# Sums of squares of the differential half in two single-pass matmuls over a split square

## What is computed

```python
def _rmsnorm(x, g):
    xf = x.astype(jnp.float32)
    y = xf * lax.rsqrt(jnp.mean(xf * xf, axis=-1, keepdims=True) + EPS)
    return (y * g.astype(jnp.float32)).astype(x.dtype)
...
    qd = _rmsnorm(df_q.reshape(b, s, DF_HEADS, 2, DF_HEAD_DIM), q_norm_g)
    kd = _rmsnorm(df_k.reshape(b, s, DF_HEADS, 2, DF_HEAD_DIM), k_norm_g)
...
    df_o = _diff_attention(q1, q2, k1, k2, vd, lam, _alibi_slopes(DF_HEADS))
    df_o = _rmsnorm(df_o, subln_g) * (1.0 - lam_init)
    df_out = _from_blocks(df_o) * jax.nn.silu(df_g.astype(jnp.float32))
```

## Time and profile before

| what | value |
|---|---|
| median of 3 runs | 1531.65 us (1530.02 to 1531.93) |
| the profiled execution | 1531.95 us |
| its span in the profile | 1530.2 us |
| TensorE busy | 1477.6 us |
| VectorE busy | 957.4 us |
| ScalarE busy | 671.5 us |

### The profile page before, as it was taken

How to read it: one execution, slowest core, us unless ns; L and a number is a source line. 1 busy time by engine, 2 the same in 40 slices (tenths; PEclk the granted TensorE clock), 3 DMA queues, 4 the chain that set the end, 5 groups by cost and what they waited for, 6 DMA issues and landing times.

```text
span 1530.2 us, 20100 instructions
## 1 busy us (share of the span) xinstructions
PE 1477.6 (97%) x7076; PEld 1156.4 (76%) x7076; DVE 957.4 (63%) x1464; ACT 671.5 (44%) x1085; POOL 66.5 (4%) x123
## 2 busy tenths in 40 slices
PE   5999899999999999999989999999999999999988
PEld 5876678888888887666767888888888766667767
DVE  6644667777776647545446777777777654456662
ACT  6544444444442225344443444444332355555661
POOL 1100000000001120000000000000111011100000
PEclk9999999999999999999999999999999999999999
DMA  6222223322236632111212322223576411111221
GB/s 239 97 69 70 83 84 107 96 96 96 96 116 222 237 126 83 67 45 42 69 42 83 110 96 96 96 96 111 199 247 212 134 55 55 56 56 55 70 97 56
DMA packets 42899, 159.16 MB, mean 104 GB/s; under 512 B 4884, under 2 KB 5140, under 8 KB 42840
## 3 DMA queue, kind: packets, MB, share of 16 engines
q1 hardware_dynamic: 33480, 126.40, 24.7%
q0 software_dynamic: 8208, 29.89, 5.9%
q10 hardware_dynamic: 1152, 2.10, 0.4%
HBM read 156.27 MB, written 2.10 MB: 103 GB/s over the span
## 4 chain that ended last, share of the span: by engine, by line
PE 86%; DVE 6%; ACT 5%; issue 2%; DMA 0%; SPq 0%; ACTq 0%; DVEq 0%
PE ps L348 18%; PE ps L350 17%; PE ps L349 17%; PE ps L364 7%; PE ps L366 7%; PE ps L365 7%; PE ps L451 2%; PE ps L521 2%; DVE wl L282 1%; PE ps L509 1%; ACT wh L276 1%; PE ps L1741 1%; DVE rbc L445 1%; PE ps L1731 1%; PE ps L1756 1%
## 5 line engine op out<-in xcount | busy, mean ns | idle before, releaser
L276 ACT CAST wh<-raw 128x1024 fp32r<-128x1024 f32 (+1 forms) x213 | 234.5, 1101 | 283.0 <-PE ps L350 247.4
L282 DVE TENSOR_TENSOR wl<-raw,wh 128x1024 fp32r<-128x1024 f32 (+1 forms) x213 | 273.3, 1283 | 99.4 <-ACT wh L276 99.2
L348 PE MATMUL ps<-xh,wh 128*128 128x512 f32 x728 | 284.3, 391 | 1.7 <-DVE wl L282 1.7
L350 PE MATMUL ps<-xh,wl 128*128 128x512 f32 x728 | 283.3, 389 | 0.0
L349 PE MATMUL ps<-xl,wh 128*128 128x512 f32 x728 | 283.2, 389 | 0.0
L364 PE MATMUL ps<-xh,wh 128*128 128x512 f32 x448 | 191.8, 428 | 2.5 <-DVE wl L282 2.5
L366 PE MATMUL ps<-xh,wl 128*128 128x512 f32 x448 | 176.3, 394 | 0.0
L365 PE MATMUL ps<-xl,wh 128*128 128x512 f32 x448 | 175.9, 393 | 0.0
L348 PEld LDWEIGHTS ps<-xh,wh 128*128 128x128 f32 x728 | 136.6, 188 | 31.1 <-DVE wl L282 2.5
L349 PEld LDWEIGHTS ps<-xl,wh 128*128 128x128 f32 x728 | 136.6, 188 | 28.9 <-issue 0.5
L350 PEld LDWEIGHTS ps<-xh,wl 128*128 128x128 f32 x728 | 136.6, 188 | 28.3
(11 more groups left out here) (271 smaller groups left out, 2152.0 us busy)
## 6 DMA issues: line engine op xcount, KB each, us to landing
raw<-w_a_f SPq DMA_DIRECT2D x44, 512.0 KB, 3.2
raw<-w_b_f SPq DMA_DIRECT2D x44, 512.0 KB, 3.2
row<-w_c_rows POOLq DMA_DIRECT2D x32, 512.0 KB, 4.6
row<-w_ada_rows POOLq DMA_DIRECT2D x24, 512.0 KB, 4.8
raw<-w_a_f SPq DMA_DIRECT2D x16, 704.0 KB, 4.1
raw<-w_b_f SPq DMA_DIRECT2D x16, 704.0 KB, 4.4
raw<-w_b_pair SPq DMA_DIRECT2D x18, 512.0 KB, 3.2
raw<-w_sb SPq DMA_DIRECT2D x16, 512.0 KB, 3.3
```

The source lines that it names most:

```text
L276: nc.scalar.copy(wh[:, s, :width], raw[:, s, :width]).then_inc(w_hi, 1)
L282: nc.vector.tensor_tensor(wl[:, s, :width], raw[:, s, :width], wh[:, s, :width].bitcast(F32), ALU.subtract).then_inc(w_lo, 1)
L348: nc.tensor.matmul(dst, a, h(k), start=(k == 0), stop=False)
L350: mm = nc.tensor.matmul(dst, b, h(k), start=False, stop=(k == total - 1))
```

## The change

The square is copied once more by ScalarE into a tile of type fp32r (`sqh`), VectorE subtracts that from the square into another (`sql`, `square_low`), and TensorE makes two fp32r matmuls, one over each, added in PSUM. The ones and the block of ones are copied into fp32r once (`plus`), on ScalarE ahead of unit 0. `square_low` stands in VectorE's order at the step of the sum: at step 0 behind the reductions, at step 4 behind L1411 and ahead of the split, at step 6 behind the reductions (or clamps, in unit 3) and ahead of the split; for the last output, behind unit 7. TensorE waits for it (`lo`) in place of the square (`sq`).

```diff
--- before.py
+++ after.py
@@ -189,6 +189,9 @@
         ptd = at("ptd", [P, 2, S], F32, 70)
         osb = at("osb", [P, S], F32, 74)
         sqd = at("sqd", [P, S], F32, 76)
+        sqh = at("sqh", [P, S], F32R, 46)
+        sql = at("sql", [P, S], F32R, 48)
+        plus = at("plus", [P, 2 * P], F32R, 54)
         ogt = at("ogt", [P, S], F32, 78)
         kal = at("kal", [68, 5 * S], BF16, 80)
         rfn = at("rfn", [P, S], F32, 85)
@@ -232,7 +235,8 @@
         c_b, c_e, c_l, c_sp, c_sc, c_p = (sem("c_" + n) for n in ("b", "e", "l", "sp", "sc", "p"))
         b_vt, b_vn = sem("b_vt"), sem("b_vn")
         sbs = {n: sem("sb_" + n) for n in ("z", "min", "e", "ln", "sp", "tri", "a", "u", "pv")}
-        dfs = {n: sem("df_" + n) for n in ("sq", "ss", "ln", "r", "n", "o1", "o2", "qg")}
+        dfs = {n: sem("df_" + n) for n in ("sq", "hi", "lo", "ss", "ln", "r", "n", "o1", "o2", "qg")}
+        k_plus = sem("k_plus")
         l_vt, l_vn, l_si, l_o, l_pr = sem("l_vt"), sem("l_vn"), sem("l_si"), sem("l_o"), sem("l_pr")
         n_x2, n_h, n_hs = sem("n_x2"), sem("n_h"), sem("n_hs")
         y_out = [sem("y_out0"), sem("y_out1")]
@@ -940,9 +944,11 @@
             act.wait_ge(ada_mod, 4)
             rounds(act, "b_f2", 4, 4, split_hi, body)
 
-            def squares(src, s_ready, v_ready):
+            def squares(k, src, s_ready, v_ready):
                 act.wait_ge(s_ready, v_ready)
                 nc.scalar.activation(sqd[:, :], src, ACT.Square).then_inc(dfs["sq"], 1)
+                act.wait_ge(dfs["sq"], k + 1)
+                nc.scalar.copy(sqh[:, :], sqd[:, :]).then_inc(dfs["hi"], 1)
 
             def unit(n, k, src=st):
 
@@ -957,10 +963,10 @@
                 n, i, p = C0["sb"] + 4 * u + l, u - 4, u % 2
                 split_hi(act, n + 2, n + 2)
                 if i >= 0 and l == 0:
-                    squares(kts[:, p, :], l_pr, 3 * u + 1)
+                    squares(n_k(i), kts[:, p, :], l_pr, 3 * u + 1)
                 if i >= 0 and l == 1:
                     unit(HD, n_k(i))
-                    squares(qts[:, p, :], l_pr, 3 * u + 2)
+                    squares(n_q(i), qts[:, p, :], l_pr, 3 * u + 2)
                 if l == 3:
                     act.wait_ge(l_vt, u + 1)
                     unit_pv(act, u - 2)
@@ -988,6 +994,8 @@
                 return f
 
             project(0, 0)
+            nc.scalar.copy(plus[:, 0:P], ones).then_inc(k_plus, 1)
+            nc.scalar.copy(plus[:, P:2 * P], bdiag).then_inc(k_plus, 1)
             norm_root(act, 5, rbc[:, :], bias=sm[:, 60:61])
             norm_root(act, 6, rfn[:, :])
             table(EXP_LN_SET)
@@ -1047,7 +1055,7 @@
                 act_pairs(exps, copy, behind_last(u))
                 if u < 7:
                     project(u + 1, 3)
-                squares(osb[:, :], dfs["o1"], u - 3)
+                squares(n_o(u - 4), osb[:, :], dfs["o1"], u - 3)
             unit(P, n_o(3), lg[0])
             mix_high(act, 7, MIXC + 7, ogt[:, :], l_o, 8)
 
@@ -1392,6 +1400,11 @@
                     nc.vector.scalar_tensor_tensor(kts[:, p, :], kts[:, p, :], col("k_norm_g_2"), drb[:, :],
                                                    ALU.mult, ALU.mult).then_inc(dfs["n"], 1)
 
+            def square_low(k):
+
+                dve.wait_ge(dfs["hi"], k + 1)
+                nc.vector.tensor_tensor(sql[:, :], sqd[:, :], sqh[:, :].bitcast(F32), ALU.subtract).then_inc(dfs["lo"], 1)
+
             def output(i):
 
                 k = n_o(i)
@@ -1410,6 +1423,12 @@
                             norm_factor(dve, 6, rfn[:, :])
                         nc.vector.scalar_tensor_tensor(xt[:, u, :], xt[:, u, :], col("final_norm", u), rfn[:, :],
                                                        ALU.mult, ALU.mult).then_inc(n_x2, 1)
+                    if u > 4 and t == 0:
+                        square_low(n_o(u - 5))
+                    if 3 <= u < 7 and t == end_step(0, 4) + 2:
+                        square_low(n_k(u - 3))
+                    if 3 <= u < 7 and t == end_step(1, 4) + 2:
+                        square_low(n_q(u - 3))
                     if u > 4 and t == 1:
                         output(u - 5)
                     if u > 4 and t == 2:
@@ -1488,6 +1507,7 @@
                 if u < 7:
                     project(u + 1, 3)
                     split(u + 1, 3)
+            square_low(n_o(3))
             output(3)
             mix_low(dve, 7, MIXC + 7, ogt[:, :])
 
@@ -1660,9 +1680,12 @@
                     pe.wait_ge(dfs["ln"], n_q(u - 4) + 1)
                 turn(pe, st, vts[:, :], l_pr, 3 * u + 3).then_inc(l_vt, 1)
 
+            ones_r, bdiag_r = plus[:, 0:P], plus[:, P:2 * P]
+
             def sums(k, m, dst=st):
-                pe.wait_ge(dfs["sq"], k + 1)
-                nc.tensor.matmul(dst[:, :], m, sqd[:, :], start=True, stop=True).then_inc(dfs["ss"], 1)
+                pe.wait_ge(dfs["lo"], k + 1)
+                nc.tensor.matmul(dst[:, :], m, sqh[:, :], start=True, stop=False)
+                nc.tensor.matmul(dst[:, :], m, sql[:, :], start=False, stop=True).then_inc(dfs["ss"], 1)
 
             OUT_EARLY = ([(j, k) for j in range(2) for k in range(6)] + [(0, 6), (1, 6)] +
                          [(j, k) for j in (2, 3) for k in range(7)])
@@ -1699,12 +1722,13 @@
                         for i in range(2 * t, 2 * t + 2):
                             out_block(*OUT_EARLY[i])
                     if u > 4 and t == 0:
-                        sums(n_o(u - 5), ones)
+                        sums(n_o(u - 5), ones_r)
                     if 3 <= u < 7 and t == end_step(0, 4) + 2:
                         pe.wait_ge(l_vn, u + 1)
-                        sums(n_k(u - 3), bdiag)
+                        pe.wait_ge(k_plus, 2)
+                        sums(n_k(u - 3), bdiag_r)
                     if 3 <= u < 7 and t == end_step(1, 4) + 2:
-                        sums(n_q(u - 3), bdiag)
+                        sums(n_q(u - 3), bdiag_r)
                 return f
 
             job(pe, [(C0["sb"], C0["sb"], KD)], J0["sb"], J0["sb"], X, XL, ready=(x_lo, X0["sb"]))
@@ -1804,7 +1828,7 @@
             for i in range(20, 23):
                 out_block(*OUT_EARLY[i])
             pe.wait_ge(att["df"]["exp"], 32)
-            sums(n_o(3), ones, lg[0])
+            sums(n_o(3), ones_r, lg[0])
             for i in range(23, 28):
                 out_block(*OUT_EARLY[i])
             for j in range(4):
```

## The result

The changed kernel takes 1541.10 us (median of 4 runs, 1538.97 to 1542.93) against 1531.79 for the kernel before: ratio 1.0061, 95% interval 1.0044 to 1.0077, so slower by 9.3 us. The forecast was slower, 1537.4 us, range 1533.8 to 1540.5. The direction was right and the size too small: the median lies 0.6 us above the range. The four runs lie in two pairs, 1538.97 and 1539.52 with a mean granted clock of 0.994, 1542.68 and 1542.93 with 0.991. The profiled execution is the fastest, 1538.97 us with a span of 1537.0.

What follows compares the result with a forecast made beforehand. TensorE's own queue was taken to set the pace. Terms of 0.9 + 3.8 + 0.4 + 0 + 0.6 gave +5.7 us; 1531.95 + 5.7 - 0.3 made 1537.4 us, range 1533.8 to 1540.5.

Steps and rivals of the forecast that it cites:

- unit 3, pair: Unit 3's key and query sums: key's 0.41 us used up waiting, query sum late behind clamps and subtraction; +0.4 us.
- unit 4, key and query: Unit 4's two sums: query sum waits about 2 us for the subtraction behind VectorE's reductions; together +1.27 us.
- units 5 and 6, key and query: Same query wait on VectorE's subtraction in units 5 and 6: +1.27 us per unit, +3.8 over units 4 to 6.
- output sums, units 5 and 6: Step 0 of units 5 and 6: TensorE waits for the subtraction behind the reductions; +0.47 us each, +0.9 in all.
- unit 7 up to the last sum: Unit 7's output sum leaves TensorE 1.1 us later, taken up by ptd waits; 0 taken, bounds 0 and +1.1 us.
- the tail: Last sum, behind unit 7, in a chain without cover: copy and subtraction come before it; +0.6 us.
- Unit 7's absorption: Claim that unit 7's 2.2 us of ptd waits take up TensorE's 1.1 us delay, so its end does not move.
- the key's 0.41: Key sums, units 4 to 6: 0.41 us saved, mostly lost on TensorE to the later weight split, kept through ScalarE's chain.
- rival 3: The clock: new 2 us idle stretches before query sums might set off lower-clock spells, 1.7 us each; 1539.1 to 1542.5 us; 10%.
- The faster rival: Subtraction always ends before TensorE comes: 11 sums save 0.41 us each, tail costs 0.6; -3.9, 1527.8 us; 5%.

Runs made afterwards that it cites:

- the waits without the saving: Changed kernel with copies, subtractions and waits kept, but each sum again one fp32 matmul over the unsplit square: 1543.10 us, ratio 1.0072 to the kernel before.
- the repetition: The changed kernel run again with no edit, five runs: 1540.95 us, ratio 1.0056 to the kernel before.
- the high half only: Changed kernel without copy, subtraction and low half: square written straight into fp32r, one single-pass matmul, less exact; 1527.11 us, ratio 0.9962 to the kernel before.
- filled runs: Changed kernel with throw-away matmuls before each query sum (two in unit 3, seven in units 4 to 6), run twice: 1539.09 us (1.0042), 1537.59 us (1.0032).

## Why the prediction was right and wrong

**The terms.** The changed kernel's profile can be set against the rows of before by the start of the same places. TensorE is 0.67 us early already at the block behind the wait at 1232.07 (the wait is the same 2.46 us there), which the change does not touch, so the terms are differences between places. A waiting sum takes 0.57 to the next instruction (1389.22 to 1389.79; forecast 0.56).

| term | forecast | by the two profiles |
|---|---|---|
| unit 3, pair | +0.4 | 1350.34 against 1350.62, -0.28, from -0.67: +0.39 |
| unit 4, key and query | +1.27 | key sum starts 0.23 early, step 6's transposes 1.04 late: +1.27 |
| units 5 and 6, key and query | +1.27 each | the same places: +1.36, +1.34 |
| output sums, units 5 and 6 | +0.47 each | unit 5: 1403.71 against 1402.29, +1.42: +0.38; unit 6: +0.32 |
| unit 7 up to the last sum | 0 (to +1.1) | from reductions to TensorE's arrival, 1475.46 to 1503.01 against 1469.40 to 1496.73: +0.22 |
| the tail | +0.6 | arrival 1496.73 to block 1502.09 against 1503.01 to 1508.91: +0.54 |
| all | +5.7 | +5.8 |
| a spell behind unit 6's query sum | 0 | from the transposes of step 6 to unit 7's reductions, 1461.65 to 1475.46 against 1457.11 to 1469.40: +1.52 |

Arrival of the last sum is its start less the wait, 1503.87 - 0.86. The places of before that are named stand in the earlier trace rows, but for 1457.11, a start of L1787. With the 0.67 us that it was early and 0.15 of small differences between the places, 5.8 and 1.5 make the 6.8 us by which this execution is longer. Unit 7's absorption held, in two parts: its ptd waits fell by 0.4 us (2.2 to 1.8) where 1.1 was forecast, and its pd waits by another 0.4 (1.3 to 0.9). Runs say the same of the whole: with the query sums left as before the loss is 0, with their subtraction moved ahead 5.7 us are back, and the two matmuls save 0.4 each. That ScalarE's chain keeps the key's 0.41, although the later weight split takes most of it on TensorE, is shown by the run with only the key sums split.

**The step that failed** is the clock: the sum takes it as 1.00 from 1335 us on, a term of 0, and leaves its fall to rival 3. That rival was priced rightly (1.7 us for a spell, 1.5 to 1.6 seen: six matmuls at 0.43 in place of 0.23 and some thin ones) but given only 10%. It is the usual case: both profiles of the changed kernel, and that of the waits without the saving, have a spell behind one or two of the three new idle stretches. Over the five repeated runs the mean clock is 0.9928 against 0.9951 before, 0.0023 of 1541 us, at most 3.5 us. It costs that much only where TensorE alone sets the pace: among the 16 runs of the kernel before, four at 0.993 took 1534.1 to 1534.3 us and three at 0.997 took 1529.9 to 1530.6, about 1 us for 0.001, and by that it is an estimate of 2.2 us. The argument against the rival was that the new stretches are shorter than the 3.41 us of the earlier trace rows; waits of 2 us were enough. The Trainium skill, TensorE: Matmul & The Clock Gate, HAM oscillation — how this bites in real kernels, has waits in a loop, longer ones than these, bring the low level back each time. The five spells behind query sums agree in kind, and the four query sums without one say that not every wait does. The terms, 5.8, and 2.2 to 3.5 for the clock make 8.0 to 9.3; 9.3 was measured first and 8.7 in the repetition. With the idle filled the kernel took 1.0032 and 1.0042 times the time before, 4.9 and 6.4 us more, around the forecast's 5.7: that the terms came out right was no luck, and that the total did not is the clock.

**A step that was missing but did not count** is that TensorE cannot keep all of its own saving at step 6. The faster rival supposed that eleven sums would each save 0.41 if the operand were never late. The runs with the query sum moved, and the one with the high half only, show that VectorE's weight split there sets a second bound just behind, so that rival was worth less than it said.

Open: why one stretch of 2 us has a spell behind it and another none. Its length alone does not decide, since 2.15 us had none and 1.97 us had one, and neither does the place, since each of the three query sums had both. Open too: how much of the spread that is left in the filled runs is the wait at 1232 us. Neither was tried alone.

## What to carry to other kernels

When an operand of the engine that bounds is made cheaper by work on another engine, find where that work stands in the other engine's queue and add what is ahead of it: here 1.3 us of reductions in front of a subtraction of 0.7 outweighed 0.4 saved. Split only where the other engines are ahead (the key sums here), and test a term by applying the edit at one kind of place at a time. Price an idle stretch of the matrix engine at its length plus the chance of a spell at the lower clock, even where it is short, and look at what the saved work had been covering.

## What the runs showed of the hardware

Idle stretches of 2.0 to 2.4 us on TensorE were followed, 1.7 us or less of work later, by some 3.4 us at the lower level (0.50 to 0.55 granted) in five of nine cases in three profiles. The fifteen stretches of 1.3 to 1.6 us in front of a query sum or a weight split, in the profiles of the five runs that move a subtraction or a sum, had none. Seven throw-away matmuls in the stretch left none in two profiles. An identical wait of 2.46 us at 1232 us had a spell behind it in the profiles of both filled runs and of the repetition, and none in that of the kernel before. The copy to fp32r took 0.62 us (L951) and the subtraction 0.68 (L1406), as the borrowed rows said (0.625 and 0.693); a 128x128 copy took 0.295.
